# Hybrid dilated-attention encoder on eight cores: sixteen halo tiles transposed by the DMA queue into staging buffers instead of by TensorE into PSUM

## The reference, cut to what matters

```
hn   = RMSNorm(x) * norm_g
proj = hn @ w_in                      # 1024 -> 9216: q, k, v for 3 head groups, gates, conv branch, merge gates
for (window, dilation) in ((128,1), (512,4), (2048,16)):
    attention of 8 heads x 64; query t sees keys t + j*dilation, |j| <= 64, with ALiBi bias
attn = sum of the three groups, weighted by their softmax denominators
a    = (silu(z_a) * attn) @ w_attn_out
c    = (silu(z_b) * gb * conv3(gc * hc)) @ w_conv_out
y    = RMSNorm(x + (sigmoid(g_a) * a + sigmoid(g_c) * c) @ w_o) * final_g
```

## Time and profile before

| | us |
|---|---|
| median of 3 runs (lowest, highest) | 1474.95 (1473.37, 1475.21) |
| time of the profiled execution | 1475.51 |
| its span on the slowest core | 1474.0 |
| TensorE (PE) busy | 1454.9 |
| VectorE (DVE) busy | 887.3 |
| ScalarE (ACT) busy | 661.9 |
| GpSimd (POOL) busy | 177.6 |

### The profile page before, as it was taken

One profiled execution on the slowest core, in us unless ns is written; L12 is line 12 of the kernel. 1 busy time (PEld: TensorE's weight loads), 2 busy tenths in 40 slices (PEclk: granted clock), 3 DMA queues, 4 the chain that ended last, 5 costly groups with the idle time before them and its releaser, 6 DMA issues.

```text
span 1474.0 us, 30550 instructions; the slowest of 8 cores (1469.1 to 1474.0 us)
## 1 busy us (share of the span) xinstructions
PE 1454.9 (99%) x13201; PEld 848.2 (58%) x13245; DVE 887.3 (60%) x1194; ACT 661.9 (45%) x1011; POOL 177.6 (12%) x320
## 2 busy tenths in 40 slices
PE   7999999999999999999999999999999999999998
PEld 5756765665655544444455767877776444444443
DVE  4677473473573896554466458394765967433357
ACT  4667455555455422443232556565655311222234
POOL 3452000000010010232011101000100100000000
PEclk9999999999999999999999999999999999999999
DMA  9673234143154141999295524425341522222157
GB/s 227 171 163 84 59 76 70 20 92 54 20 101 78 28 74 22 170 161 205 41 300 152 118 61 66 93 37 73 69 66 31 86 52 42 31 34 44 22 195 261
DMA packets 109994, 138.16 MB, mean 94 GB/s; under 512 B 69362, under 2 KB 69394, under 8 KB 109860
## 3 DMA queue, kind: packets, MB, share of 16 engines
q0 software_dynamic: 27728, 54.65, 22.8%
q1 hardware_dynamic: 82132, 81.56, 21.9%
HBM read 145.97 MB, written 23.66 MB: 115 GB/s over the span
## 4 chain that ended last, share of the span: by engine, by line
PE 96%; DMA 3%; DVE 1%; SPq 0%; issue 0%; ACT 0%; DVEq 0%; ACTq 0%; POOLq 0%
PE ps L456 87%; PE ps L468 8%; DMA Y<-xw 2%; DMA wbf<-wblk 1%; PE ps L483 1%; SPq L487 0%; DVE Y L420 0%; DVE hnT L444 0%; DVE Y L411 0%; ACT Y L443 0%; DVE Y L444 0%; DVEq L1383 0%; ACT Y L407 0%; ACT stat L1191 0%; PE ps L690 0%
## 5 line engine op out<-in xcount | busy, mean ns | idle before, releaser
L456 PE MATMUL ps<-hnT,wbf 128*128 128x512 bf16 (+4 forms) x5648 | 1025.0, 338 | 4.7 <-DMA wbf<-wblk 3.5
L456 PEld LDWEIGHTS ps<-hnT,wbf 128*128 128x128 bf16 x5648 | 523.2, 98 | 444.1 <-DMA wbf<-wblk 3.8
L407 ACT ACTIVATE Y<-ps 128x1024 bf16<-128x1024 f32 (+1 forms) x292 | 240.8, 872 | 192.4 <-PE ps L456 143.9
L443 ACT ACTIVATE Y<-ps 128x512 bf16<-128x512 f32 (+1 forms) x304 | 181.1, 597 | 275.1 <-PE ps L456 253.7
L411 DVE TENSOR_TENSOR Y<-ps,Y 128x512 f32<-128x512 f32 (+1 forms) x196 | 125.7, 673 | 203.8 <-PE ps L468 170.5
L420 DVE SCALAR_TENSOR_TENSOR Y<-Y,ps 128x512 f32<-128x512 f32 x192 | 130.8, 683 | 167.9 <-PE ps L456 149.0
L487 POOL DMA_DIRECT2D wbf<-wblk x160 | 86.9, 544 | 962.3 <-PE ps L456 945.9
L407 ACT ACTIVATE Y<-ps,cf 128x512 f32<-128x512 f32 x128 | 87.6, 686 | 218.2 <-PE ps L456 205.3
L411 DVE TENSOR_TENSOR Y<-Y,et 128x1024 bf16<-128x1024 bf16 x192 | 129.8, 685 | 15.6 <-ACT Y L407 11.3
L407 ACT ACTIVATE Y<-Y 128x1024 bf16<-128x1024 f32 (+3 forms) x83 | 85.9, 1035 | 115.6 <-DVE Y L420 86.0
L468 PEld LDWEIGHTS ps<-Y 64*128 64x128 bf16 x4640 | 114.5, 94 | 31.4 <-issue 26.3
(11 more groups left out here) (48 smaller groups left out, 424.0 us busy)
## 6 DMA issues: line engine op xcount, KB each, us to landing
wbf<-wblk POOLq DMA_DIRECT2D x160, 256.0 KB, 4.9
Y<-xw SPq DMA_DIRECT2D x56, 512.0 KB, 7.9
Y<-xw SPq DMA_DIRECT2D x48, 256.0 KB, 7.0
y<-Y POOLq DMA_DIRECT2D x16, 512.0 KB, 4.3
y<-Y SPq DMA_DIRECT2D x15, 512.0 KB, 5.1
Y<-wblk POOLq DMA_DIRECT2D x16, 256.0 KB, 7.5
et<-etab SPq DMA_DIRECT2D x8, 384.0 KB, 3.7
cv<-Y SPq DMA_DIRECT2D x4, 768.0 KB, 5.1
```

The costliest lines, as they stand in the source:

```text
L407: R.add("act", [lambda e: e.activation(out=out.a, in_=in_.a, func=func, scale=scale, **kw)], c_act(in_.n) + (0.2 if accum is not None else ...
L443: return e.activation(out=out.a, in_=in_.a, func=AF.Copy)
L456: fns = [(lambda e, m=m: e.matmul(m[0].a, lhsT=m[1].a, rhs=m[2].a, start=m[3], stop=m[4])) for m in mms]
```

## The change

`ln_halo` takes the place of `ln_span` for all sixteen halo tiles of the first half.

- The rows of a tile are loaded residue by residue (four residues outside, n rows inside) instead of token block by token block. The number of loads, their bytes and the 4 KB of a row stay.
- The scaled tile is not transposed by PE: one DMA transpose of 128 rows x 1024 channels on SP's queue writes it into one of four staging buffers `hst` (2 KB each, at 104 to 112 KB of the work area). The same space holds `ca`, the accumulator of the first convolution (`conv_buf[1]`), which `conv_end` writes and reads.
- The copies into `hnT` (one or two for a tile, 24 in all, as before) read the staging buffer in place of a PSUM bank, in runs of n columns.
- The loads have kind "h" in place of "late": the planner expects them 2.5 us earlier.

```diff
+        hst = [yb(104 + 2 * i, 2048, BF16) for i in range(4)]
...
+        def ln_halo(c, i0s, n):
+
+            loads = [(16 * i0 + c, [(4, 4), (16, n)], 4 * n * k, 4 * n) for k, i0 in enumerate(i0s)]
+            st = oldest(hst)
+            ln_tile(loads, [(st, 0, 128, 0, 128)], xt0, xn0, gb0, jk0, None, kind="h")
+            for k, i0 in enumerate(i0s):
+                copy(hnT.ap(1024 * c + i0, [[WIN, 8], [256, 4], [1, n]]), st.ap(4 * n * k, [[128, 8], [n, 4], [1, n]]),
+                     dcost=0.1 + 0.0128 * n)
...
-                    ln_span(j, (48, 192), 16, ln_bank())
+                    ln_halo(j, (48, 192), 16)
...
-                        ln_span(c, i0s, n, next_bank())
+                        ln_halo(c, i0s, n)
```

## The result

The changed kernel took 1531.14 us (median of 4 runs, 1530.87 to 1532.98) where the kernel before took 1474.95 us beside it: the ratio is 1.0387, with a 95% interval of 1.0366 to 1.0407. It is 56 us slower. The prediction was 1469.3 us, with the range ending at 1476.0: the sign was wrong, and none of the rivals came near.

What follows compares the result with a forecast made beforehand. PE was taken to bound the kernel, busy 1454.9 of 1474.0 us. Transposes -7.2 and new idle time +1.5 gave -5.7 us, from the 1474.95 median to 1469.3 us; range 1464.1 to 1476.0.

Steps and rivals of the forecast that it cites:

- The loads keep number, bytes and 4 KB rows; only the order of rows changes. Counted at nothing.: Halo loads of x on SP's queue: reordering their rows was claimed to cost 0 us.
- the hold observed: Kernel before, 60 to 160 us: ACT stood 3.04 us for a load before a Square; PE went on 1.72 us late.
- 128 transposes, -7.2 us: Sixteen halo tiles of eight transposes leave PE, each worth its chain distance of 0.056 us: 7.2 us less.
- Copies at nothing: 24 copies into hnT on ACT and DVE: 4 to 5 us of work saved, hidden by idle time, counted as nothing.
- Issue on SP, 1.3 us: Sixteen DMA transposes on SP's queue: 1.3 us each (upper bound 2.5), 21 us, fitting into 77 us of waiting.
- Landing, 5.5 us: DMA transposes of halo tiles: each taken to land at 5.5 us, between 3.1 and 11.7.
- DMA time of a tile, 1.2 to 2.1 us: DMA engines, 60 to 160 us: a full transpose takes 1.2 to 2.1 us, all sixteen 20 to 33 us.
- Holds, +1.5 us: Stretch from 60 to 160 us: engines waiting for landings raise PE idle time from 2.7 to 4.2 us.
- the holds eat the gain: Rival, six groups of attention transposes: 1 to 1.4 us each, 6 to 8 us; 1474 us, no measurable change; chance 0.16.
- No consumer of the halo is late: First tiles 6 us later against some 14 us of room, next ones over 10 us of room: cost nothing.
- Transposes and loads delay each other: Rival, SP's queue and DMA engines: landings at 11.7 us, six groups cost 10.3 us, net +3.1, 1478.1 us; chance 0.09.
- The signs listed as proof of error: Wrong if stretch idle exceeds 8 us, PE waits for hnT itself, or DMA share reaches 1 and weights come late.

Runs made afterwards that it cites:

- the first experiment: Changed kernel with halo loads back in the old row order, DMA transposes and staging kept, copies picking every fourth column: 1473.17 us, ratio 0.9994.
- late loads in the old order: Changed kernel with halo loads in the old row order and planned as late (without kind "h"): 1483.79 us (1474.39 to 1490.98), ratio 1.0093.
- start tiles alone: Changed kernel with old row order, only the four first tiles by DMA transposes, attention's twelve on PE: 1481.20, 1481.71, 1500.82, 1503.32 us, ratio 1.0113.
- the last version: Changed kernel with old row order, only twelve attention tiles by DMA, loads planned late, transposes 4 us later, groups one place earlier: 1469.42 us, ratio 0.9966.

## Why the prediction was wrong

**The step that failed:** "The loads keep number, bytes and 4 KB rows; only the order of rows changes. Counted at nothing." It was priced by what is moved, not by how the access pattern spreads it over engines. In its place the runs show 36 us for the order alone and 56 with the transposes behind it. I had looked for the costs of the transposes and passed over a line of the diff in which two pairs change places. No row of the kernel before has a load with an outer dimension of 4, so its price was to be bounded from both sides by rows, as was done for the transposes. An upper end was at hand: each of the 24 loads late enough for the hold observed, 24 x 1.72 us or 41 us. That would have covered the 36 us, though not the 56. No end above nothing was set, and so the range could not hold the time.

**Term by term.**

- 128 transposes, -7.2 us: right (7.1 where they are left out). The chain's distance, not the duration, was the right row.
- Copies at nothing: right by their duration. The copy on DVE took 423 ns, a little over the 0.35 to 0.4 us said, and ACT gained nothing. In the old order of rows, picking every fourth column, the same copy took DVE 685 ns: that difference is all that the new order gains, and it is small beside 36 us.
- Issue on SP, 1.3 us: right with loads on all engines (median 1.27), and 1.8 in the median, up to 14.5, in the kernel after. "The queue has room" was read from SP's waiting time, 77 us; but an issue that blocks for 13 us in front of the loads isn't bounded by room.
- Landing, 5.5 us: too high in the median with loads on all engines (3.4 in the first experiment), but one there took 13.0, over the upper bound of 11.7; too low in the change (6.5, up to 21.0).
- DMA time of a tile, 1.2 to 2.1 us: near, as far as the share tells. It is 0.86 in the stretch with sixteen DMA transposes in the old order, 0.65 without halo transposes and 0.55 in the kernel before: 21 to 31 us, or 1.3 to 1.9 each.
- Holds, +1.5 us: mis-sized even without the new order. In the first experiment idle time in the stretch was 9.3 us, 6.6 more than before, on the slowest core, and 3.5 more on average. In time that is the rival "the holds eat the gain" (1474 us): the change without its order of rows took 1473.17. Its mechanism is only partly that rival's, since the longest wait there is for the halo itself.
- "No consumer of the halo is late": wrong, and the second step that failed. The four first tiles were said to be read from 91.7 us on, with 14 us of room. That is `edge1`; `edge0` reads them at 81.35 us, with 2.4 us of room; a tile that comes 6 us later, by the prediction's own count, is 3.6 us late there. With the old order of rows PE waits there 3.7 to 7.0 us, and in the kernel after 11.9 to 14.7 us, on every core. Its timeline has PE held for 14.41 us by a copy of halo that waited for a transpose:

```profile
92.12 0.50 DVE L445 COPY hnT<-Y 128x512 bf16<-128x512 bf16 x2 [4.85 <-DMA Y<-Y]
...
92.67 1.89 PE L457 MATMUL ps<-hnT,wbf 128*128 128x128 bf16 x16 [14.41 <-DVE hnT L445]
```

**The rivals.** "Transposes and loads delay each other" had the right sign and half of the mechanism: copies held, scalings held (8.0 us of DVE's waits), loads behind on SP late. Its price was 3.1 us, since each group was given the one hold observed, 1.72 us, and the loads their old speed. Its point of decision, 10.2 us of new idle time, was passed five times over. The signs listed as proof of error came: idle time above 8 us, PE waiting for hnT, a DMA share of 0.96. Weights did land later (13.4 us in the median from 60 to 240 us, 5.5 before), but PE never waited for one there.

**The clock** was in no term. It stayed at 1.00 in the stretch before; after idle stretches it fell to the lower level, and some 12 us of PE's busy time came from it (5.3 us more on average over the cores, and the 7.1 that the transposes had taken). The long stalls here were dearer than their own length.

**Open:** the scatter of two kernels (late loads in the old order; start tiles alone), how the loss of the twelve tiles divides between late loads and held copies, and what part of the last version's gain is the earlier place.

## What to carry to other kernels

Read a changed access pattern as a change of speed, even where bytes, rows and number of transfers stay: look at which dimension is outermost, and how many entries it has (16 were enough here, 4 cost 36 us). When work is moved from the busiest engine to DMA, its old time is a sure gain, but every landing that an in-order engine waits for must be planned at the time the trace shows, or the gain returns as idle time; start it early rather than just in time. Look for the first reader of what is moved in the order of PE's work, by the columns it reads: here it stood 10 us before the one that had been looked at. And price a queue by what may block its head, not by its idle share.

## What was not expected of the hardware

- A load of 4 KB rows whose outer dimension is 4 ran at a DMA share of 0.23 to 0.27 and 86 to 111 GB/s; with 16 or more rows outermost, in the kernel before, 0.87 and 270 GB/s in a burst.
- A DMA transpose of 128 x 1024 behind such loads held the issuing queue for up to 14.5 us, against 1.27 in the median with loads on all engines. One stretch of SP's timeline of the kernel after:

```profile
70.30 1.23 SPq L492 DMA_TRANSPOSE Y<-Y  x1
71.58 1.74 SPq L488 DMA_DIRECT2D Y<-xw  x3
...
73.95 13.41 SPq L492 DMA_TRANSPOSE Y<-Y  x1
87.40 4.77 SPq L488 DMA_DIRECT2D Y<-xw  x4
```

  The transpose at 70.30 passed in 1.23 us; the one behind three more loads took 13.41, and four loads of x stood behind it.
- In quiet a full transpose (eight blocks) lands after 3.0 us, as the 64-column ones did.
- PE had no work for 14.4 us (to 92.67 us); its granted clock was 0.56 from 80 to 90 us and 0.50, the lower level, from 90 to 100 us, though it worked again.
